# Delta rule of a hybrid decoder step: when the next tile's decay, the gate rows, z's second chunk and the solved blocks come

## The chip, the cores and the metric

One core of one Trainium2 chip runs the whole program in one launch. The metric is the time of one execution in device microseconds (us), as the median of several runs. TensorE (PE) multiplies matrices, VectorE (DVE) and ScalarE (ACT) work elementwise and can read TensorE's results in PSUM, GpSimd (POOL) works elementwise on SBUF, and SyncE (SP) issues DMAs. Each engine takes its instructions in order; semaphores tie the engines together.

## The reference

The program is one inference step of a two-layer trunk: a layer with sparse attention, a layer with gated DeltaNet, an MLP behind each. Tokens are 512 of a prompt and 8 sequences of 8 new tokens. Only the DeltaNet layer is touched. Its core, per head (16 value heads, keys and values of width 128, state 128 x 128):

```python
gam = jnp.cumsum(gc, axis=-1)                      # gc: log decay per token, in a chunk
diff = gam[..., :, None] - gam[..., None, :]
decay = jnp.where(incl, jnp.exp(jnp.where(incl, diff, 0.0)), 0.0)
a_mat = jnp.where(strict, bc[..., :, None] * jnp.einsum('...id,...jd->...ij', kc, kc) * decay, 0.0)
tinv = lax.linalg.triangular_solve(eye + a_mat, jnp.broadcast_to(eye, a_mat.shape), left_side=True, lower=True)
value = tinv @ (vc * bc[..., None])
kcum = tinv @ (kc * (bc * jnp.exp(gam))[..., None])
qk = jnp.einsum('...id,...jd->...ij', qc, kc) * decay
def step(s, xs):                                   # over chunks
    u = val - kcm @ s
    o = qd @ s + qkm @ u
    s = s * gl + jnp.swapaxes(kd, -1, -2) @ u
...
o = o * lax.rsqrt(jnp.mean(o * o, axis=-1, keepdims=True) + RMS_EPS) * norm_w * jax.nn.silu(zh)
y = o.reshape(n, t, GDN_V_W) @ w_out               # z = x @ w_z, the output gate
```

The states that enter and leave (`state_ssm`, one per sequence and head) are inputs and outputs.

## The kernel before

The DeltaNet layer is two stages. `gdn_in_stage` projects, convolves and normalises q, k and v in 16 weight units (n = 0 to 15); beside that POOL inverts the 16 x 16 diagonal blocks of the first four heads (`block_inverses`, a generator whose steps it takes between other work). SP writes the solved blocks to DRAM with `block_inverses_out`, 16 DMAs, and loads the first four z weight units into the ring of four slots. A barrier ends the stage.

`gdn_stage` is the delta rule. It runs four passes, `hg` 0 to 3, of four heads each. A pass has four prompt tiles of 128 tokens, i = 0 to 3, and then the eight sequences as one block of 64 tokens. Tiles alternate between two sets of buffers and PSUM banks (0 to 2 for even tiles, 3 to 5 for odd ones); z's products take pairs of banks, pair 2 being banks 4 and 5 and pair 3 banks 6 and 7. Each engine's order is written out by hand, in one function per engine, with counters per tile for the steps.

A tile goes so:

- SP loads its gate rows (`rows_load`, 256 KB into `a`), the 16 x 16 inverses (`t_load`, `inverse_load`) and the grown gates (`grown_load`).
- POOL subtracts and masks (`decay_gaps`, L3397 and L3400) and scales keys and queries by the grown gates (`grown_keys`, L3412 and L3414).
- ACT takes exp of `a` (`decay`, L3853), copies the turned values out of PSUM (`values`, L3859), scales the turned keys (`late_keys`, L3864). exp, silu and sqrt come from different tables, which an ACT_TABLE_LOAD changes; copy and square need no change.
- TensorE turns values and multiplies keys and queries (`first_products`, L3519 and L3526), turns keys (`keys_turned`, L3533). DVE makes `a` from the products (`keys`, L4007 and L4011).
- `join` grows the inverse from 16 to 32 to 64 to 128 in steps that alternate between TensorE and DVE or ACT: p16 (L3545), q16 and s16 (L3552, L3556), p32 (L3562), q32 and s32 (L3567, L3571), p64 (L3576), s64 (L3582). Between q32 and p64 ACT copies (`joined_32`, L3871 and L3874), after s64 again (`joined_64`, L3879).
- `use` applies the tile with the state: keys by state (L3599), queries by state (L3605), value (L3617), state (L3622), output (L3628). ACT squares the output (`square`, L3887), DVE sums, TensorE turns it (L3639), ACT writes it out (`out`, L3897).

TensorE runs the use of tile i between the join steps of tile i+1 and the first products of tile i+2. In ACT's loop over i before the change the order is

```python
late_keys(w[i + 1]); root(*last); decay(w[i + 2])          # last: norm of tile i - 1
out(*last, hg, i - 1); joined_32(w[i + 1]); square(*norm_of(hg, i), hg, i)
values(w[i + 2]); joined_64(w[i + 1])
```

The keys of the next pass are multiplied in 32 x 32 blocks by TensorE (`block_keys`, L3076), copied by ACT (L3953), sent through DRAM by SP and inverted by POOL.

After the tiles come the sequences: `seq_front`, then products with the eight states of each head j (L3814), then for each j two products (L3834) that DVE adds to the state (L4198), which POOL has scaled before (L3494). DVE spreads values for them (`by_sequence`, L4180). At the end SP stores the 2 MB of states (L3335).

z, the gate, is projected in the same pass as filler for TensorE's waits: `z_products` yields 32 pieces of a pass, 4 chunks c of 8 pieces (L3730, each 4 records), of which the last 8 (c = 3) are left for the next pass's start, except in pass 3. `Z_PAIR` says which pair of banks a chunk uses, ACT's `silu_z` (L3926) empties it and counts `z_out`. In pass 0 there is no such rest, and `keep_busy` multiplies ones instead (L123).

Four of the 16 q and k chunks ("units" 12 to 15) are brought to unit length in this stage by DVE (`unit_length`: a reciprocal, L4068, and a product, L4070), in the order 12, 13, 15, 14.

## Time and profile before

| | |
|---|---|
| median of 3 runs | 2309.18 us (2308.81 to 2311.12) |
| profiled execution, its own time | 2311.1 us |
| its span, first to last instruction | 2309.4 us |
| TensorE busy | 2182.4 us, 94% of the span |
| POOL, DVE, ACT busy | 1124.2, 1008.4, 577.0 us |
| mean granted TensorE clock | 0.974 of full speed |
| delta-rule stage, first instruction to the next stage's | 1243.5 to 1736.1 us |

How to read it: busy time is the time in which an engine had an instruction running. TensorE's matmuls are pipelined, so 94% does not mean that it does 94% of what it could. The granted clock is 1.0 at 2.4 GHz and 0.5 at 1.2 GHz. Waits and timelines tell what an engine waited for before an instruction: the brackets at the end of a row give the idle time and the instruction that ended it. "x4" counts records of one line that stand together.

### The profile page before, as it was taken

How to read it: one execution, taken by the hardware profiler on the slowest of the kernel's cores; microseconds unless marked ns; L12 is line 12 of the kernel's file. 1: busy time of each engine (PE TensorE's matmuls, PEld its weight loads, DVE VectorE, ACT ScalarE, POOL GpSimd, SP SyncE). 2: the span in 40 equal slices, each digit the busy share in tenths (PEclk: the TensorE clock that was granted, in tenths of full speed). 3: DMA queues.
4: the chain of work that ended last, by engine and by line, in shares of the span. 5: the costliest groups of instructions: out<-in, count | busy, mean ns of one | idle time of the engine just before them, and what ended most of it. 6: DMA issues, size and time to landing. Idle time of an engine off the chain costs nothing. (4 is left out here: it accounts for less than half of the span.)

```text
span 2309.4 us, 33163 instructions
## 1 busy us (share of the span) xinstructions
PE 2182.4 (94%) x12590; PEld 1617.2 (70%) x12590; DVE 1008.4 (44%) x1879; ACT 577.0 (25%) x1292; POOL 1124.2 (49%) x1075
## 2 busy tenths in 40 slices
PE   9898999899999999999998898989899999999997
PEld 7675555476777777767775767676767767777776
DVE  5343676336330341357886544343443163313422
ACT  2103577501000000135554424343320010000011
POOL 3212555257654565365695243525237276644653
PEclk9999799999999999999999999999999999999999
DMA  9825001911212221432223314242303122122211
GB/s 331 223 77 184 1 2 45 327 63 66 73 59 99 80 74 73 144 90 75 68 74 73 89 42 133 54 131 56 124 24 132 73 92 73 55 76 107 73 73 41
DMA packets 125912, 216.47 MB, mean 94 GB/s; under 512 B 73602, under 2 KB 96002, under 8 KB 109762
## 3 DMA queue, kind: packets, MB, share of 16 engines
q1 hardware_dynamic: 119234, 197.13, 25.9%
q0 software_dynamic: 3088, 14.03, 1.8%
q10 hardware_dynamic: 3440, 3.25, 0.4%
q8 instruction: 102, 1.67, 0.3%
q14 instruction: 48, 0.39, 0.1%
HBM read 185.08 MB, written 37.55 MB: 96 GB/s over the span
## 5 line engine op out<-in xcount | busy, mean ns | idle before, releaser
L2014 PE MATMUL ps<-xn,ring 128*128 128x288 f32 x768 | 198.8, 407 | 5.4 <-DVE xn L2117 3.2
L2014 PE MATMUL ps<-hid,ring 128*128 128x288 f32 x768 | 192.8, 406 | 0.0
L2014 PEld LDWEIGHTS ps<-xn,ring 128*128 128x128 f32 x768 | 145.3, 190 | 48.3 <-DVE xn L2117 5.9
L2014 PEld LDWEIGHTS ps<-hid,ring 128*128 128x128 f32 x768 | 145.6, 190 | 40.7 <-ACT p L2051 0.8
L2097 POOL TENSOR_TENSOR prod<-prod,rstd 128x1152 f32<-128x1152 f32 x32 | 83.9, 2621 | 179.6 <-DVE prod L2181 163.3
L2051 ACT ACTIVATE p<-ps 128x288 f32<-128x288 f32 x48 | 19.7, 410 | 597.4 <-PE ps L2014 597.4
L3730 PE MATMUL ps<-xn,ring 128*128 128x288 f32 x512 | 149.2, 429 | 5.9 <-PE ps L3834 4.0
L1122 POOL TENSOR_SCALAR ring<-ring,fac 128x128 f32<-128x128 f32 (+2 forms) x96 | 92.2, 976 | 88.1 <-DVE fac L1551 88.1
L2014 PE MATMUL ps<-x_sum,wsum 128*128 128x288 f32 x512 | 130.5, 407 | 3.4 <-DVE x_sum L2121 1.9
L2071 POOL TENSOR_TENSOR wsum<-ring 128x512 f32<-128x512 f32 x64 | 81.9, 1279 | 99.9 <-DMA ring<-in_w_mlp 92.0
L2014 PE MATMUL ps<-hid_sum,wsum 128*128 128x288 f32 x512 | 128.4, 407 | 0.2
L3730 PEld LDWEIGHTS ps<-xn,ring 128*128 128x128 f32 x512 | 93.3, 196 | 44.6 <-issue 22.6
L2014 PEld LDWEIGHTS ps<-x_sum,wsum 128*128 128x128 f32 x512 | 96.8, 190 | 32.0 <-issue 3.2
L2014 PEld LDWEIGHTS ps<-hid_sum,wsum 128*128 128x128 f32 x512 | 96.9, 190 | 28.3 <-POOL ring L2072 1.9
L2899 DVE SCALAR_TENSOR_TENSOR x<-x,gi_convw 128x600 f32<-128x600 f32 x90 | 92.4, 1026 | 30.6 <-ACT x L2693 28.3
L2171 DVE TENSOR_TENSOR u<-p,ps 128x288 f32<-128x288 f32 x48 | 21.7, 452 | 169.1 <-PE ps L2014 169.1
L2162 DVE TENSOR_TENSOR u<-p,ps 128x288 f32<-128x288 f32 x48 | 21.8, 453 | 159.3 <-PE ps L2014 159.3
L2076 POOL TENSOR_TENSOR wsum<-ring,wsum 128x512 f32<-128x512 f32 x64 | 87.9, 1374 | 5.0
L2072 POOL TENSOR_TENSOR ring<-ring 128x512 f32<-128x512 f32 x64 | 89.1, 1392 | 0.0
L3397 POOL TENSOR_TENSOR gdn_tiles<-gdn_tiles,gdn_upto_tok 128x512 f32<-128x512 f32 x16 | 16.6, 1040 | 145.4 <-DMA gdn_tiles<-gate_rows_scratch 145.2
L2074 POOL TENSOR_TENSOR wsum<-wsum,ring 128x512 f32<-128x512 f32 x64 | 82.9, 1295 | 0.0
L1382 ACT ACTIVATE ring<-ps,nmax 128x128 f32<-128x128 f32 (+3 forms) x128 | 66.1, 523 | 58.3 <-DVE nmax L1499 58.3
(597 smaller groups left out, 4650.8 us busy)
## 6 DMA issues: line engine op xcount, KB each, us to landing
ring<-in_w_mlp SPq DMA_DIRECT2D x64, 1024.0 KB, 4.9
ring<-in_w_gdn_in SPq DMA_DIRECT2D x16, 1024.0 KB, 4.9
ring<-in_w_nsa_in SPq DMA_DIRECT2D x9, 1024.0 KB, 17.4
ring<-in_w_gdn_z SPq DMA_DIRECT2D x8, 1024.0 KB, 5.0
x<-in_seq_state SPq DMA_DIRECT2D x4, 2048.0 KB
out_seq_state<-x SPq DMA_DIRECT2D x4, 2048.0 KB, 12.1
ring<-in_w_gdn_out SPq DMA_DIRECT2D x8, 1024.0 KB, 5.6
out_win_old<-in_win_rows POOLq DMA_DIRECT2D x1, 8064.0 KB, 46.5
```

What stands on the lines that cost most here:

```text
L1122: nc.gpsimd.tensor_scalar(p, p, fac[:, job % 2, half, i:i + 1], None, ALU.mult).then_inc(scaled, 1)
L1382: nc.scalar.activation(prob[job % 3][half][:, p_at(i):p_at(i) + width(i)], S.ps[:, score_bank(k, half), 0:width(i)], ACT.Exp, bias=nmax[:, ...
L2014: mm = nc.tensor.matmul(S.ps[:, base + BANK[p], 0:HT], stationary(p, blk.units[pair // 4], pair % 4), moving(blk.kind, p, pair), start=pai ...
L2071: g.tensor_tensor(wsum[:, slot, 0], quad[:, slot, 2], quad[:, slot, 3], ALU.add).then_inc(w_summed, 1)
L2072: g.tensor_tensor(quad[:, slot, 2], quad[:, slot, 0], quad[:, slot, 2], ALU.subtract).then_inc(w_summed, 1)
L2074: g.tensor_tensor(wsum[:, slot, 1], wsum[:, slot, 0], quad[:, slot, 0], ALU.subtract).then_inc(w_summed, 1)
L2076: g.tensor_tensor(wsum[:, slot, 2], quad[:, slot, 1], wsum[:, slot, 1], ALU.subtract).then_inc(w_summed, 1)
L2097: g.tensor_tensor(prod[:, i % 2], prod[:, i % 2], S.rstd[:, 1:2, :].broadcast_to([128, 2, T]), ALU.mult).then_inc(normal, 1)
L2162: v.tensor_tensor(u2[:, n % 2], p1[:, n % 2], b, ALU.add).then_inc(u2_set, 1)
L2171: v.tensor_tensor(u3[:, n % 2], p1[:, n % 2], b, ALU.add).then_inc(u3_set, 1)
L2899: i = v.scalar_tensor_tensor(out=c_, in0=p[:, t:t + CV], scalar=tap(t), in1=c_, op0=ALU.mult, op1=ALU.add)
L3730: mm = nc.tensor.matmul(S.pairs[:, Z_PAIR[c], half, :], S.ring[:, unit % SLOTS, k * 256 + (c % 2) * 128:k * 256 + (c % 2) * 128 + 128], S. ...
```

## The change

All of it is in the order of work; no arithmetic and no size of a transfer changes.

- SP, `gdn_in_stage`: the 16 stores of the first solved blocks are issued after the third z unit is loaded, not after the fourth and the convolution's rows.
- SP, `gdn_stage`, passes 1 to 3: the wait for z's last chunk and the ring load go from the head of the pass to behind tile 2's gate rows and inverses. The store of the states no longer waits for z's chunk.
- z's chunk 1 uses pair 2 and chunk 2 pair 3; the waits of TensorE go with them. `first_products` waits for `silu_z` only for tile 1, and for chunk 1 instead of chunk 2.
- ACT: `late_keys(w[1])` goes ahead of the last silu of the pass before, `decay(w[i + 2])` goes behind the square and right ahead of `values(w[i + 2])`. At the end of a pass tile 0's decay goes behind a silu.
- POOL: the next pass's tile 0 is prepared between the second and third state, not before the first. At the start, two of eight scalings of x precede the tiles instead of three.
- TensorE: `block_keys` goes from between p16 and q16 to behind the state product; pass 0 has four ones products instead of six at one place.
- DVE: unit 13's reciprocal and product go between tile 0's join steps (`unit_length` is split).
- Two constants are written by name; their values stay (2 and 3).

```diff
@@ gdn_in_stage, sync
                 if u == 2:
                     conv_out(2, 4, 8, 14)
+                    sp.wait_ge(blank_out, 32)
+                    block_inverses_out(sp, blocks, place, 0)
             z.prefetched = True
             conv_out(3, 4, 6, 15)
-            sp.wait_ge(blank_out, 32)
-            block_inverses_out(sp, blocks, place, 0)
             sp.wait_ge(last_set, 32)
@@ gdn_stage
-        Z_PAIR = (3, 3, 2, 3)
+        Z_PAIR = (3, 2, 3, 3)
@@ sync
                 else:
-                    sp.wait_ge(zd.product, 4 * hg)
-                    ring_load(2 * hg + 3)
                     sp.wait_ge(seq_add, hg * 8)
                     sp.dma_start(S.out["seq_state"][hg - 1], seq_state).then_inc(seq_out, 16)
                 wait_step(sp, C[0], "pe", w[0].job, "p64")
                 rows_load(w[2])
                 t_load(w[2])
+                if hg:
+                    sp.wait_ge(zd.product, 4 * hg)
+                    ring_load(2 * hg + 3)
                 wait_step(sp, C[0], "pe", w[0].job, "value")
                 grown_load(w[2])
                 inverse_load(w[2])
@@ gpsimd
-            scaled(0, 3)
+            scaled(0, 2)
             for i in range(2):
                 decay_gaps(tile(0, i))
                 grown_keys(tile(0, i))
-            scaled(3, KD)
+            scaled(2, KD)
...
                 if hg < 3:
-                    for i in (1, 0):
-                        decay_gaps(tile(hg + 1, i))
-                        grown_keys(tile(hg + 1, i))
+                    decay_gaps(tile(hg + 1, 1))
+                    grown_keys(tile(hg + 1, 1))
                 wait_step(pool, Q, "pe", hg, "value")
                 pool.wait_ge(seq_in, 16 * hg + 16)
                 for j in range(4):
+                    if j == 2 and hg < 3:
+                        decay_gaps(tile(hg + 1, 0))
+                        grown_keys(tile(hg + 1, 0))
                     g.tensor_tensor(seq_state[:, j], seq_state[:, j], seq_total(S, hg, j), ALU.mult).then_inc(seq_decayed, 1)
@@ tensor, first_products
                     wait_step(pe, Q, "act", w.hg)
-                    pe.wait_ge(z_out, 4 * w.hg - 1)
+                    if w.i == 1:
+                        pe.wait_ge(z_out, 4 * w.hg - 2)
@@ tensor, z_products
-                            elif c == 2:
+                            elif c == 1:
                                 wait_step(pe, C[1], "vec", 2 * hg + 2)
                                 wait_step(pe, N[1], "act", 2 * hg + 2)
                             else:
-                                pe.wait_ge(z_out, 4 * hg + (1 if c == 1 else 2))
+                                pe.wait_ge(z_out, 4 * hg + (1 if c == 2 else 3))
@@ tensor, the passes
                 first_products(first)
-                pause(1, 6)
+                pause(1, 4)
...
                     next(used)
-                    if i == 0 and hg < 3:
-                        pe.wait_ge(z_out, 4 * hg)
-                        if hg == 2:
-                            pe.wait_ge(late_unit, LATE)
-                        block_keys(S, hg + 1, lambda i, kh: ...).then_inc(blocks.keys_mm, 1)
                     next(joins, None)
                     next(used)
                     next(joins, None)
...
                     next(used)
+                    if i == 0 and hg < 3:
+                        (the same five lines)
                     if last:
                         turn(last[0], last[2], last[3])
@@ scalar
                 joined_64(w[0])
+                late_keys(w[1])
                 if hg:
                     silu_z(hg - 1, 3)
                 for i in range(PT):
                     last = norm_before(hg, i) if i else None
-                    if w[i + 1]:
+                    if i and w[i + 1]:
                         late_keys(w[i + 1])
                     if last:
                         root(*last)
-                    if w[i + 2]:
-                        decay(w[i + 2])
...
                     square(*norm_of(hg, i), hg, i)
                     if w[i + 2]:
+                        decay(w[i + 2])
                         values(w[i + 2])
...
                 if hg < 3:
-                    for i in (1, 0):
-                        decay(tile(hg + 1, i))
+                    decay(tile(hg + 1, 1))
                 silu_z(hg, 1)
+                if hg < 3:
+                    decay(tile(hg + 1, 0))
                 out(*norm_of(hg, PT), hg, PT)
                 silu_z(hg, 2)
@@ vector
+            def unit_inverse(e):
+                v.reciprocal(late_root(S, e), late_root(S, e)).then_inc(late_inverse, 1)
+
             def unit_length(e):
                 c, at = unit_chunk(e), late_root(S, e)
-                v.reciprocal(at, at).then_inc(late_inverse, 1)
...
                 if hg == 0:
+                    unit_inverse(12)
                     unit_length(12)
-                    unit_length(13)
                 keys(w[0])
                 joins = join(w[0])
                 next(joins)
+                if hg == 0:
+                    unit_inverse(13)
                 next(joins)
                 keys(w[1])
                 next(joins)
+                if hg == 0:
+                    unit_length(13)
                 next(joins)
```

## Rows read from the trace of the kernel before

**Rows 1.** TensorE's waits, 1230 to 1740 us: total us, times, longest.
```profile
PE ps L3576 <- ACT gdn_tiles L3871: 15.8, 3, 5.6
PE ps L3545 <- ACT gdn_tiles L3864: 6.2, 3, 2.1
...
PE ps L3834 <- DVE x L4198: 4.9, 3, 3.1
...
PE ps L3519 <- ACT gdn_shared L3926: 2.6, 3, 0.9
...
PE ps L3730 <- ACT gdn_shared L3926: 2.0, 4, 0.5
```

**Rows 2.** Timeline of TensorE, pass 1, around tile 1's 64-join: start, us, what.
```profile
1404.73 1.02 PE L3576 MATMUL ps<-gdn_tiles 64*64 64x64 f32 x8 [4.86 <-ACT gdn_tiles L3871]
...
1410.71 0.68 PE L3545 MATMUL ps<-gdn_tiles 64*64 64x64 f32 x16 [0.38 <-DVE gdn_tiles L4011]
```

**Rows 3.** Timeline of TensorE, pass 0, the same place, and the block keys.
```profile
1272.40 0.76 PE L3076 MATMUL ps<-gdn_qkv 128*32 128x32 f32 x64
...
1279.36 0.68 PE L3576 MATMUL ps<-gdn_tiles 64*64 64x64 f32 x8
...
1283.76 0.68 PE L3545 MATMUL ps<-gdn_tiles 64*64 64x64 f32 x16 [0.38 <-DVE gdn_tiles L4011]
```

**Rows 4.** Busy time and granted clock (PEclk), pass 1, behind the wait.
```profile
1405.00:1408.00 3.00, 3.00 (x19) 2.88 (x18) 0.43 (x1) 1.44 (x3) 1.26 (x1) 0.50 0.24 71
```

**Rows 5.** Timeline of ScalarE, pass 1, tiles 1 and 2.
```profile
1388.39 0.63 ACT L3926 ACTIVATE gdn_shared<-ps 128x576 f32<-128x576 f32 x1
1388.92 1.11 ACT L3864 ACTIVATE gdn_tiles<-ps,cst 128x128 f32<-128x128 f32 x4
1390.05 1.28 ACT L3853 ACT_TABLE_LOAD   x1
1403.75 0.63 ACT L3853 ACTIVATE gdn_tiles<-gdn_tiles 128x512 f32<-128x512 f32 x1 [12.42 <-POOL gdn_tiles L3400]
```

**Rows 6.** Timeline of GpSimd, pass 1, tile 2's decay gap.
```profile
1401.34 1.04 POOL L3397 TENSOR_TENSOR gdn_tiles<-gdn_tiles,gdn_upto_tok 128x512 f32<-128x512 f32 x1 [43.59 <-DMA gdn_tiles<-gate_rows_scratch]
```

**Rows 7.** DMA issues, 1387.4 to 1389.8 us (pass 1): KB, us to landing.
```profile
out_seq_state<-x SPq DMA_DIRECT2D x1, 2048.0 KB, 12.3
...
gdn_tiles<-gate_rows_scratch SPq DMA_DIRECT2D x1, 256.0 KB, 12.9
```

**Rows 8.** DMA issues of 1268.5 to 1269.4 us, pass 0.
```profile
gdn_tiles<-gate_rows_scratch SPq DMA_DIRECT2D x1, 256.0 KB, 3.2
```

**Rows 9.** Timeline of TensorE, pass 1, first and third state product.
```profile
1470.28 1.13 PE L3834 MATMUL ps<-gdn_tiles 32*128 32x512 f32 x4
...
1480.44 1.13 PE L3834 MATMUL ps<-gdn_tiles 32*128 32x512 f32 x4
```

**Rows 10.** Timeline of TensorE, pass 3, first and third state product.
```profile
1709.13 1.13 PE L3834 MATMUL ps<-gdn_tiles 32*128 32x512 f32 x4
...
1716.23 1.13 PE L3834 MATMUL ps<-gdn_tiles 32*128 32x512 f32 x4
```

**Rows 11.** Timeline of VectorE, last state adds of pass 0, first of pass 1.
```profile
1365.76 1.29 DVE L4198 TENSOR_TENSOR x<-x,ps 128x512 f32<-128x512 f32 x2 [2.14 <-PE ps L3834]
...
1473.83 1.28 DVE L4198 TENSOR_TENSOR x<-x,ps 128x512 f32<-128x512 f32 x2 [3.31 <-POOL x L3494]
```

**Rows 12.** Timeline of VectorE, start of the stage.
```profile
1254.97 0.68 DVE L4007 TENSOR_TENSOR gdn_tiles<-ps,gdn_tiles 128x512 f32<-128x512 f32 x1
```

**Rows 13.** Timeline of ScalarE, start of the stage.
```profile
1250.67 0.63 ACT L3853 ACTIVATE gdn_tiles<-gdn_tiles 128x512 f32<-128x512 f32 x1 [5.49 <-POOL gdn_tiles L3400]
```

**Rows 14.** Timeline of ScalarE, pass 0, copies around tile 1.
```profile
1293.84 0.60 ACT L3859 ACTIVATE gdn_tiles<-ps 128x512 f32<-128x512 f32 x1 [0.59 <-PE ps L3519]
1295.34 0.38 ACT L3879 ACTIVATE gdn_tiles<-ps 64x256 f32<-64x256 f32 x1 [0.90 <-PE ps L3582]
```

**Rows 15.** Waits of SP's queue, 1239 to 1246 us.
```profile
SPq L115 <- PEq L115: 0.7, 1, 0.7
```

More of the change, by code:

```diff
@@ L3355, in _ @@
                     if hg == 0:
-                        sp.wait_ge(late_unit, 2)
+                        sp.wait_ge(late_unit, LATE_ORDER.index(13) + 1)
                     else:
@@ L3775, in _ @@
                     next(used)
-                    if i == 0 and hg < 3:
-                        pe.wait_ge(z_out, 4 * hg)
-                        if hg == 2:
-                            pe.wait_ge(late_unit, LATE)
-                        block_keys(S, hg + 1, lambda i, kh: S.ps[:, 6, 64 * i + 32 * kh:64 * i + 32 * kh + 32]).then_inc(blocks.keys_mm, 1)
                     next(joins, None)
@@ L3787, in _ @@
                     next(used)
+                    if i == 0 and hg < 3:
+                        pe.wait_ge(z_out, 4 * hg)
+                        if hg == 2:
+                            pe.wait_ge(late_unit, LATE)
+                        block_keys(S, hg + 1, lambda i, kh: S.ps[:, 6, 64 * i + 32 * kh:64 * i + 32 * kh + 32]).then_inc(blocks.keys_mm, 1)
                     if last:
@@ L3922, in silu_z @@
                 if n == 0:
-                    act.wait_ge(late_unit, 3)
+                    act.wait_ge(late_unit, LATE_ORDER.index(15) + 1)
                 if hg:
@@ L4154, in _ @@
                     if (hg, i) == (0, 2):
+                        unit_inverse(15)
                         unit_length(15)
@@ L4185, in _ @@
                 if hg == 0:
+                    unit_inverse(14)
                     unit_length(14)
```

## The prediction

> **What bounds the kernel now.** The delta-rule stage runs four passes (hg 0 to 3), in each four prompt tiles (0 to 3) and then the eight sequences. TensorE's order is written out by hand, so a wait in it moves everything behind it. I read first TensorE's own waits over this stage [rows 1]: the reader is to see that few lines carry the idle time, and that most of these occur three times, once in each pass after the first. The largest is L3576 (the 64-join of tile 1, "p64"), 15.8 us in three waits for ACT L3871.
>
> Second, TensorE in time: in pass 1, p64 starts after 4.86 us idle and the next tile's first join 5.98 us after that [rows 2]; in pass 0, with no wait, the same distance is 4.40 us [rows 3]. The difference, 1.58 us, is the granted clock: just after the idle stretch it is 0.50, the lower level, 1.2 GHz [rows 4]. So a long wait costs about a third more than its idle time.
>
> Third, who is late. ACT L3871 is a small copy that queues behind tile 2's decay (L3853). The decay waited 12.42 us for POOL [rows 5], POOL for its DMA of gate rows [rows 6], and that DMA took 12.9 us to land because SP issued it behind a 1 MB ring load and the 2 MB state store, which itself took 12.3 us [rows 7]. In pass 0, with nothing ahead of it, the same load lands in 3.2 us [rows 8].
>
> Fourth, the sequence states at the end of a pass: in pass 1 TensorE goes from its first state product (1470.28) to the third (1480.44) in 10.16 us [rows 9], in pass 3, which has no next tile to prepare, in 7.10 us (1709.13 to 1716.23) [rows 10]. In pass 1 VectorE's first add waits 3.31 us for POOL [rows 11], which does both decays of the next pass before the first state.
>
> Fifth, the stage's start: VectorE's keys of tile 0 (L4007) begin at 1254.97, right behind two length units [rows 12], though the decay that they need was there at 1250.67 + 0.63 = 1251.30 [rows 13].
>
> **The change part by part** (us, summed over the stage).
>
> Gate rows ahead, decay behind the copy. SP no longer holds the state store until z's product is through; it can go when the last state add is done, at 1367.05 (1365.76 + 1.29 [rows 11]). The rows were issued at about 1388.4 (1401.34 - 12.9 [rows 6, 7]), 21 us after that, so the store's 12.3 us are over by then even if p64 comes some us earlier. The ring load goes behind tile 2's rows. So I take the 3.2 us landing. ACT does the decay after the copies, so p64 waits for neither: 15.8 saved [rows 1], and the slow clock behind it, 3 x 1.58 = 4.7 [rows 2, 3]. Were the rows late again, the decay would hold the value copy behind it instead, 2.4 a pass. That is worked out so: rows issued at 1388.4 that land 3.2 later are masked by 1393.9 (1.04 [rows 6] and some 1.3); p64 without its wait runs at 1399.9 (1404.73 - 4.86 [rows 2]), and the decay is due some 1.3 behind it, so 7.3 of the 9.7 (12.9 - 3.2) are covered. What is queued behind the moved ring load on SP are the grown rows and inverse of tile 2; they are issued after tile 0's value product and have a whole tile of cover.
>
> Tile 1's keys before silu. L3545 waits 6.2 in three for ACT's late keys L3864, which stand behind one silu [rows 1, 5]. They start at 1388.92 where the silu starts at 1388.39 [rows 5]; swapped, they gain 0.53 a pass, 1.6. The remaining wait of 1.5 comes from the 64-join copy ahead of both, which stays. Bounds: 1.6, and 1.6 + 3 x 1.5 if the shorter wait no longer lowers the clock; I take the first, since the state loop too loses 3.06 around waits of 0.9 ((4.9 - 3.1)/2 [rows 1]), most of it clock.
>
> The first products' wait for silu (2.6 in three, 0.87 each) is dropped for tile 0; the wait moves to z's last chunk behind these products, which cover it: 2.6 saved. In pass 3 nothing stands between z's third and fourth chunk, which now share a pair of banks: the same wait, 0.87, is new there. Bounds 0.6 (the silu alone [rows 5]) and 2.4 (with a clock fall of 1.5 more). On z's second chunk, moved to the other pair, the wait of 0.5 a pass goes: 2.0 saved [rows 1]. Its new wait, for tile 3's output copy, comes before the silu in ACT's order, so it is met.
>
> Tile 0's decay into the state loop. POOL's first state is scaled two instructions earlier (1.04 for the gap [rows 6], somewhat more for the mask), 2.3 of the 3.31 that VectorE waits [rows 11]. In passes 1 and 2 this should bring the 10.16 to the 7.10 of pass 3: 2 x 3.06 = 6.1 saved [rows 9, 10]. In pass 0 VectorE's own length unit is in front and stays; nothing. Bounds 0 to 6.1; I take 6.1, as pass 3 shows the loop without the decays. The third state now waits for the decay, but TensorE's third product is 10 us in, POOL's third state about 8.5. ACT's silu, exp, silu there adds two table loads a pass, while ACT waits for TensorE's turn.
>
> Start of the stage. Half of unit 12 and 13's work leaves the front. At most 1254.97 - 1251.30 = 3.7 is gained before the decay limits [rows 12, 13]; but the second unit's reciprocal comes back between two join steps, partly beside tile 1's products, and may open a new gap there that lowers the clock (1.5). Two ones products fewer shorten TensorE's filler so that it can follow. Bounds 1.5 to 3.7; I take 3.0. POOL's rows land at about the time when its third scale ended, so scaling two instead of three gives 0.3 at most, inside this.
>
> Costs. The block keys (L3076, 0.76 [rows 3]) leave a place where TensorE waits for VectorE anyway and go to one where it doesn't: 3 x 0.76 = 2.3 (bounds 0 and 2.3). The decay behind the square needs exp's table (1.28) and itself 0.63 [rows 5] on a path where ACT has 0.59 and 0.90 to spare [rows 14]: 0.4 left at least, 1.3 if only the first gap counts, and I take 0.55, near the lower, as the copy's reader runs later still. It applies to tile 1's turn in four passes and tile 0's in three: 3.9 (bounds 2.9 and 9.1).
>
> The Trainium skill speaks against this part: "ScalarE: Activation LUTs", section "What ACT_TABLE_LOAD costs", adds a drain of about 1.38 us to each load of 1.28. By it the seven loads would cost 9.7 more and the sum would be 19. The rows show the load at 1390.05, right as the keys end (1388.92 + 1.11) [rows 5], with no drain before it; the trace decides.
>
> Early store of solved blocks: SP at the stage's start waited 0.7 for TensorE [rows 15], so SP's 16 stores weren't what ended the stage before; nothing gained, and z's fourth unit, now behind them, is not used before pass 1. If TensorE had been ready, they would give 0.7 at most.
>
> Sum: 15.8 + 4.7 + 1.6 + 2.6 + 2.0 + 6.1 + 3.0 - 2.3 - 3.9 - 0.9 = 28.7. The profiled execution took 2311.1, 1.9 over the median 2309.2; the sum is a difference inside the stage and is taken off the median: 2280.5.
>
> **The rivals.**
> A, as above: 2280.5.
> B, the gate rows are as late as before or the state loop keeps its pace: TensorE's wait returns at the value copy (3 x 2.4 = 7.2) or the 6.1 is missing. For it: the rows still follow the 2 MB store on one queue; against it, the store starts so much earlier. 2287 to 2288, both 2294.
> C, the clock stays up after the shortened waits before tile 1's first join: 4.5 more, 2276. For it: those waits fall by a quarter; against it, waits of 0.9 sufficed in the state loop.
> D, slower. ACT now holds the value copy and the 64-join copy of the next tile behind the decay, which is in the path of every tile. Its input has 7.3 us of cover; each us beyond costs one us in every pass. To use up 28.7 the rows would have to land 7.3 + 28.7/3 = 16.9 us later than at 3.2, at 20.1; from there the time passes 2309. Against it: the latest in this stage is 12.9, with 3 MB ahead [rows 7]. At 24 us: 2321.
> E, the change doesn't do what it says, the waits only change their line: TensorE's copies, turns and keys wait for the same ACT, so the 20.5 of p64 go and return as waits at keys and first joins, with the 6.1 missing too: within 5 us of before, 2305 to 2309.
> F, each exp load on the path stops ACT for twice its row, 1.28 more: 7 x 1.28 = 9.0, 2289.5. Against it: ACT's instructions stand close around the load at 1390.05 [rows 5]. The Trainium skill's page named above is where such a rule stands.
>
> **How the numbers follow.** A 0.60, B 0.16, C 0.11, D 0.05, E 0.05, F 0.03. A's own range by the bounds: gains lower by up to 1.5 (start) and 1.5 (last wait), higher by 0.7 and 2.3: 2277 to 2284. With B's single cases, C and F, and with costs at 9.1 (5 more), the range that leaves out D, E, both of B together and little of the rest is 2271 (C with its bounds) to 2293. A measurement of this kernel tells 0.2% (4.6 us) from no change. Faster: A, B, C, F and part of E, 0.91; same: the rest of E, 0.04; slower: D, 0.05.
>
> **What would show it.** In the profile after: L3576's 15.8 gone, and with it the half clock behind; tile 2's rows landing in 3 to 4 us in passes 1 to 3, and the state store issued before p64; L3545 still waiting about 1.5 three times; exp loads behind the square and waits of about 0.5 at L3533 or L3545; the state loops of passes 1 and 2 at about 7 us; the first join of the stage near 1254 instead of 1256.87; a new wait near 0.9 before z's last chunk in pass 3. Wrong it would be if ACT's value copy (L3859) waits for the decay and TensorE for it, or if the state loop keeps its 10 us.

## The result and the profile after

| | before | changed |
|---|---|---|
| median | 2308.99 us (2307.80 to 2311.12, 4 runs) | 2270.40 us (2264.56 to 2273.84, 4 runs) |
| ratio | | 0.9829, 95% interval 0.9804 to 0.9854 |
| the same kernel in two later series | 2307.20, 2307.57 | 2275.69 and 2274.63; 0.9869 (0.9850 to 0.9888) and 0.9862 (0.9847 to 0.9877) |

The forecast was 2280.5, a gain of 28.7 us. Measured were 38.6 us in the first series and 31.5 and 32.9 in the later ones. The first series lies 0.6 us below the lower end of the forecast's range (2271 to 2293), the two later ones inside it. The signs and the places were right, the sum was too small by 3 to 10 us.

In the shown execution 10.5 us of the difference lie ahead of the delta-rule stage, which begins at 1234.24 and not at 1244.75 us, and 37.4 inside it: from its first product to the next stage's first it takes 454.1 us after (1234.24 to 1688.36) and 491.5 before (1244.75 to 1736.23).

TensorE's waits over the stage, of the changed kernel (us in total, times, longest). Its line numbers are up to 13 higher: L3545 is now L3549, L3576 is L3580, L3834 is L3838, L3864 is L3868:

```profile
PE ps L3549 <- ACT gdn_tiles L3868: 4.6, 3, 1.5
PE ps L3556 <- DVE gdn_tiles L4025: 4.0, 7, 0.9
...
PE ps L3537 <- ACT gdn_tiles L3863: 3.0, 7, 0.4
...
PE ps L3838 <- DVE x L4211: 2.4, 1, 2.4
...
PE ps L3734 <- ACT gdn_shared L3930: 1.1, 2, 0.8
```

Against [rows 1]: p64's 15.8 us are gone, and so is the wait of the first products for silu. The wait for tile 1's late keys is 1.5 and not 2.06, as forecast. New are the wait for the value copy behind the exp load (L3537, 0.4 in seven turns) and longer ones at q16 (L3556). TensorE in pass 1, around tile 1's joins, and in pass 3 ahead of z's last chunk:

```profile
1368.48 0.68 PE L3580 MATMUL ps<-gdn_tiles 64*64 64x64 f32 x8
...
1372.45 0.68 PE L3549 MATMUL ps<-gdn_tiles 64*64 64x64 f32 x16 [1.52 <-ACT gdn_tiles L3868]
...
1380.61 0.68 PE L3580 MATMUL ps<-gdn_tiles 64*64 64x64 f32 x8
...
1383.79 0.44 PE L3537 MATMUL ps<-cst,gdn_qkv 128*128 128x128 f32 x2 [0.42 <-ACT gdn_tiles L3863]
...
1677.59 2.66 PE L3734 MATMUL ps<-xn,ring 128*128 128x288 f32 x10 [0.83 <-ACT gdn_shared L3930]
```

From p64 of tile 0 to p64 of tile 1 it is 12.13 us (1368.48 to 1380.61); before it was 19.10. Who made room for that: SP's issue of tile 2's rows, GpSimd behind them, and the landing times of that stretch:

```profile
1350.94 0.37 SPq L3333 DMA_DIRECT2D out_seq_state<-x  x1
1369.18 0.33 SPq L3306 DMA_DIRECT2D gdn_tiles<-gate_rows_scratch  x1
...
1372.71 1.04 POOL L3398 TENSOR_TENSOR gdn_tiles<-gdn_tiles,gdn_upto_tok 128x512 f32<-128x512 f32 x1 [28.78 <-DMA gdn_tiles<-gate_rows_scratch]
...
out_seq_state<-x SPq DMA_DIRECT2D x1, 2048.0 KB, 6.3
...
gdn_tiles<-gate_rows_scratch SPq DMA_DIRECT2D x3, 256.0 KB, 3.5
```

The state store is issued 18 us ahead of the rows and over in 6.3 (12.3 before [rows 7]); the rows land in 3.5, not 12.9. ScalarE in the same place:

```profile
1371.24 1.11 ACT L3868 ACTIVATE gdn_tiles<-ps,cst 128x128 f32<-128x128 f32 x4
1372.24 0.64 ACT L3930 ACTIVATE gdn_shared<-ps 128x576 f32<-128x576 f32 x1
...
1380.72 0.60 ACT L3891 ACTIVATE x<-ps 128x512 f32<-128x512 f32 x1 [0.53 <-PE ps L3632]
1381.33 1.28 ACT L3857 ACT_TABLE_LOAD   x1
1382.62 0.63 ACT L3857 ACTIVATE gdn_tiles<-gdn_tiles 128x512 f32<-128x512 f32 x1
1383.16 0.58 ACT L3863 ACTIVATE gdn_tiles<-ps 128x512 f32<-128x512 f32 x1
```

Between the late copies and the 32-join copies ACT is idle for 6 us; the decay that could run there now runs behind the square. The state loop of pass 1, first to third product, takes 6.99 us (10.16 before [rows 9], 7.10 in pass 3 [rows 10]):

```profile
1444.46 1.13 PE L3838 MATMUL ps<-gdn_tiles 32*128 32x512 f32 x4
...
1451.45 1.13 PE L3838 MATMUL ps<-gdn_tiles 32*128 32x512 f32 x4
```

### The profile page after: what moved, and what is told of

Its sections match the earlier page's. It is cut to its first block and busy times, and to the rows that moved or that the text cites. A ratio compares the mean times of both kernels' runs of the same rounds, so it can differ in the third digit from the quotient of the medians.

```text
span 2262.9 us, 33160 instructions
## 1 busy us (share of the span) xinstructions
PE 2156.3 (95%) x12586; PEld 1600.4 (71%) x12586; DVE 1007.3 (45%) x1879; ACT 582.7 (26%) x1298; POOL 1125.2 (50%) x1075
## 5 line engine op out<-in xcount | busy, mean ns | idle before, releaser
L2162 DVE TENSOR_TENSOR u<-p,ps 128x288 f32<-128x288 f32 x48 | 21.8, 454 | 159.3 <-PE ps L2014 159.3
L1382 ACT ACTIVATE ring<-ps,nmax 128x128 f32<-128x128 f32 (+3 forms) x128 | 66.1, 523 | 55.3 <-DVE nmax L1499 55.3
L2474 POOL TENSOR_TENSOR x<-gi_prod,rstd 128x1024 f32<-128x1024 f32 (+1 forms) x16 | 36.7, 2293 | 69.6 <-DVE gi_prod L3011 65.3
```

Of the source, the lines that this page charges most:

```text
L1382: nc.scalar.activation(prob[job % 3][half][:, p_at(i):p_at(i) + width(i)], S.ps[:, score_bank(k, half), 0:width(i)], ACT.Exp, bias=nmax[:, ...
L2474: eng.tensor_tensor(p[:, first:last, 3:3 + TP], prod[:, first:last, 0:TP], S.rstd[:, 1:2, 0:TP].broadcast_to([128, m, TP]), ALU.mult).then ...
```

## The experiments

Medians of kernels in one series are compared with each other; finer things are read from stage lengths and stretches in the profiles, since executions differ by several us ahead of the stage (the first experiment).

**The changed kernel, twice more.**

> The changed kernel once more, nothing edited. In its first profile the delta-rule stage begins 10.5 us earlier than in the kernel before (first product at 1234.24 against 1244.75), although little of the diff runs ahead of the stage. Theory 1, chance: the clock's falls ahead of the stage differ from execution to execution; then the stage begins some us later here (1236 to 1245) and the median is 2268 to 2274, while the stage's own length, 454.1 us from its first product to the next stage's first, stays within 2 us. Theory 2, the diff does it (solved blocks stored earlier): the stage begins at 1233 to 1236 again, and so it does in each kernel with the early store.

> The changed kernel unedited, beside the next kernel on one chip. Theory: 2268 to 2277, the stage 454 to 456 us.

Measured: 2275.69 and 2274.63 us, the first above its 2268 to 2274. The stage begins at 1245.57 and 1242.07 and takes 454.7 and 458.5. So theory 2 is wrong: the same program starts the stage anywhere from 1234 to 1246. Most of the 10.5 us were chance: 6.8 of them stand before any changed line has run, where the stage ahead begins (TensorE's first L2664 at 959.6 us in the shown execution, 967.5 and 963.9 in the repetitions, 966.4 in the kernel before). What differs is the granted clock. Busy time by engine (PE, PEld, DVE, ACT, POOL), then the granted clock, DMA share and GB/s, of the shown execution in its first 600 us:

```profile
0.00:300.00 300.00, 277.45 (x1422) 194.54 (x1423) 143.81 (x364) 87.80 (x229) 94.24 (x162) 0.95 0.49 157
300.00:600.00 300.00, 286.20 (x2103) 183.58 (x2102) 155.86 (x400) 118.43 (x338) 164.04 (x143) 1.00 0.29 104
```

and of the repetition, with the same work:

```profile
0.00:300.00 300.00, 276.71 (x1393) 194.45 (x1393) 140.36 (x347) 84.29 (x219) 90.98 (x159) 0.93 0.49 157
300.00:600.00 300.00, 286.92 (x2100) 181.16 (x2097) 159.06 (x411) 121.78 (x348) 161.57 (x143) 0.98 0.29 103
```

The expected stage length held once and not the second time; the reason is in the next experiment.

**Late keys of tile 1 back behind silu.**

```diff
-                late_keys(w[1])
                 if hg:
                     silu_z(hg - 1, 3)
                 for i in range(PT):
-                    if i and w[i + 1]:
+                    if w[i + 1]:
                         late_keys(w[i + 1])
```

> The changed kernel with one edit undone: ACT's late keys of tile 1 stand behind z's last silu again. Theory of the prediction: the wait at the first join of tile 1 goes from 1.5 to 2.06 us in three passes, 1.6 us slower. Rival (the clock): a wait of 1.5 us leaves the clock up in two of three passes and one of 2.06 lowers it in all three; then 1.6 + 2 x 1.5 = 4.6 us slower, and p64 of tile 0 to p64 of tile 1 takes 13.3 to 14 us in each of passes 1 to 3, where the changed kernel takes 12.13, 13.38 and 11.44.

Measured: 2278.82 us, 3.1 more than the changed kernel in the same series. The stage takes 461.5, which is 7 us longer than in the first two profiles of the changed kernel and 3 longer than in the third. p64 of tile 0 to p64 of tile 1 takes 14.94, 14.96 and 14.24 us, where the changed kernel with the clock up takes 12.13, 12.13 and 11.44: 8.4 in all, of which 1.6 is idle time and 6.8 the clock. TensorE in pass 2, and the clock there (the column behind the five engines):

```profile
1494.36 1.12 PE L3549 MATMUL ps<-gdn_tiles 64*64 64x64 f32 x16 [2.06 <-ACT gdn_tiles L3868]
```

```profile
1494.00:1495.00 1.00, 0.64 (x12) 0.67 (x14) 0.00 (x0) 0.26 (x2) 0.49 (x1) 0.50 1.20 451
...
1498.00:1500.00 2.00, 2.00 (x10) 1.77 (x12) 0.84 (x2) 0.00 (x0) 0.00 (x0) 0.50 0.00 0
```

The rival holds, and for this stretch its price was still too low; the medians (3.1 us) lie between the two. I looked at the clock behind this wait in passes 1 to 3 of every profile, these runs' and the kernels' below. Behind waits of 2.06 us it fell to 0.50 in 13 of 15 (three of three in the kernel before); behind waits of 1.52 in 9 of 21: one, one and two of three in the three executions of the changed kernel; behind waits of 0.3 in none of 6. The three passes of one execution need not be independent: in one kernel all three fell. A fall costs 1.2 to 2.6 us in this stretch. In the shown execution it fell in pass 2 alone, at 1481:

```profile
1480.00:1481.00 1.00, 0.88 (x30) 0.88 (x32) 0.22 (x2) 0.00 (x0) 0.97 (x1) 1.00 0.99 418
1481.00:1482.00 1.00, 1.00 (x13) 0.89 (x10) 0.90 (x3) 0.00 (x0) 0.95 (x1) 0.55 0.61 254
1482.00:1483.00 1.00, 1.00 (x7) 1.00 (x5) 0.21 (x1) 0.00 (x0) 0.31 (x1) 0.50 0.04 16
```

**SP's part alone, in the kernel before** (only the `@@ sync` part of the diff: the wait for z's chunk and the ring load behind tile 2's rows).

> The kernel before with SP's part alone: in passes 1 to 3 the wait for z's last chunk and the ring load go behind tile 2's rows; ACT's order is as before. Theory 1 (the rows alone were late, the decay's place does not matter): the rows land 3.5 us after their issue, POOL takes 2.3 more, and ACT decays them some 2 us before the 32-join; p64's 15.8 us of waiting go and the slow clock behind them, 20 us faster, 2285 to 2289, with none of the 4 to 6 us that the decay behind the square costs. Theory 2 (both parts are needed): p64 of tile 1 still waits 1 us or more in each pass, and the gain is under 15 us.

Measured: 2286.37 us, 0.9903 (0.9875 to 0.9931), the stage 466.1. Theory 1 holds: the row of p64's wait is gone. ACT's decay, at its old place, waits 1.12 us for GpSimd and is still 3.17 us ahead of the 32-join:

```profile
1397.98 0.63 ACT L3854 ACTIVATE gdn_tiles<-gdn_tiles 128x512 f32<-128x512 f32 x1 [1.12 <-POOL gdn_tiles L3401]
1401.78 0.27 ACT L3872 ACTIVATE gdn_tiles<-ps 32x128 f32<-32x128 f32 x1 [3.17 <-PE ps L3568]
```

So the rows' place in SP's queue is worth some 22 us by itself, two thirds of the change. (Its late keys wait 2.06 us, and here the clock stayed up in two of three passes; why here and not in the kernel before stays open.)

**ACT's part alone, in the kernel before.**

```diff
-                    if w[i + 2]:
-                        decay(w[i + 2])
...
                     if w[i + 2]:
+                        decay(w[i + 2])
                         values(w[i + 2])
```

> The kernel before with ACT's part alone: the decay of tile i + 2 stands behind the square, ahead of the value copy; the rows are as late as before (12.9 us to land). Theory of the prediction (rival B worked out): p64 no longer waits, but the value copy behind the decay does, 2.4 us in each of three passes, and the exp load costs 3.9 to 6; so 20.5 - 7.2 - 5 = 8 us faster, 2299 to 2301. Rival E (the waits only change their line): within 3 us of before.

Measured: 2299.04 us, 0.9956 (0.9941 to 0.9970), 9.65 us faster. Rival B's mechanism, worked out in the prediction, appears, with waits of 2.3 to 2.9 us in the three passes where 2.4 was worked out:

```profile
PE ps L3533 <- ACT gdn_tiles L3859: 9.6, 7, 2.9
```

With the rows late, the decay's new place gives about half of what the rows' early issue gives (9.65 of 22), and the rest of the wait comes back at the value copy.

**The decay back at its old place, in the changed kernel.**

```diff
                         root(*last)
+                    if w[i + 2]:
+                        decay(w[i + 2])
...
-                        decay(w[i + 2])
                         values(w[i + 2])
```

> The changed kernel with ACT's decay of tile i + 2 back at its old place, ahead of the output copy and of the 32-join copies; the rows still come early. Theory of the prediction (the exp load behind the square is a cost of 0.55 in seven turns, 3.9 us): 4 to 6 us faster, since the waits of 0.4 before the turned keys and of 0.84 before q16 go and POOL is done before ACT comes to it (rows land in 3.5 us, POOL takes 2.3 more). Rival (the place of the decay is what removed p64's wait): p64 of tile 1 waits again in passes 1 to 3, 1 us or more each, and the time is the same or slower.

Measured: 2268.20 us against 2275.69 of the changed kernel in the same series, 7.5 faster where 4 to 6 were expected; the stage takes 448.9 against 454.7. The stretches that hold the moved exp load, p64 of tile 1 to p64 of tile 3 in four passes, sum to 106.6 us, and to 109.2 to 110.4 in the three profiles of the changed kernel: the load behind the square costs 2.6 to 3.9 (3.9 forecast). Of the rest, 1.4 us is the clock, which did not fall behind the late keys here and fell once in that profile of the changed kernel. p64 does not wait. So the new place gained nothing once the rows were early.

**Tile 0's decay back ahead of the states** (GpSimd and ACT prepare both tiles before the first state, as before).

> The changed kernel with the decay of the next pass's tile 0 undone on POOL and ACT: both tiles' gaps and grown keys ahead of the first state, both decays ahead of z's second silu. Theory of the prediction: the loop over the states goes from 7.0 back to 10.2 us in passes 1 and 2, 6.1 us in all, and pass 0 is as in the changed kernel (11.6), as VectorE's length unit is in front there. Rival: pass 0 loses too, 1.7 us more (13.3 as before), so that the stage goes from 454.5 to 462 us.

Measured: 2282.68 us, the stage 468.6: 14 us longer than in the first two profiles of the changed kernel, more than either theory. Waits of TensorE in the state loops, the second product of pass 1, and the clock behind it:

```profile
PE ps L3836 <- DVE x L4208: 6.8, 3, 3.7
```

```profile
1458.21 1.99 PE L3836 MATMUL ps<-gdn_tiles 32*128 32x512 f32 x4 [1.52 <-DVE x L4208]
```

```profile
1460.00:1464.00 4.00, 3.70 (x9) 2.53 (x8) 3.92 (x4) 0.00 (x0) 3.40 (x2) 0.50 0.96 295
1464.00:1468.00 4.00, 3.81 (x9) 1.38 (x8) 1.21 (x2) 0.00 (x0) 0.00 (x0) 0.50 0.00 0
```

From first to third product it is 14.17, 11.41 and 10.23 us in passes 0 to 2, against 11.60, 6.99 and 7.00 in the shown execution of the changed kernel. The waits grew by 4.4 in all (6.8 for 2.4), 1.5 in each of passes 1 and 2; the rest is the clock: in pass 1 TensorE is busy for 7.5 of the 8 us from 1460 to 1468 at the lower level. Pass 1 is slower here than in the kernel before (10.16), so this profile may price the part too high. Pass 0 loses too, so the rival's point holds. There VectorE is in front, and two of its instructions ahead of the second product take longer beside GpSimd's work: unit 14's product (1.74 us for 1.26) and the spread (`by_sequence`, L4189 here and L4192 in the changed kernel), which meets a scaling of the states here:

```profile
1343.76 2.36 DVE L4189 TENSOR_TENSOR gdn_tiles<-gdn_tiles,cst 64x512 f32<-64x512 f32 x1
```

and in the changed kernel, where GpSimd has turned to tile 0's gap by then, a shorter instruction:

```profile
1336.91 1.03 POOL L3398 TENSOR_TENSOR gdn_tiles<-gdn_tiles,gdn_upto_tok 128x512 f32<-128x512 f32 x1
...
1337.01 1.48 DVE L4192 TENSOR_TENSOR gdn_tiles<-gdn_tiles,cst 64x512 f32<-64x512 f32 x1
...
1339.61 0.67 DVE L4192 TENSOR_TENSOR gdn_tiles<-gdn_tiles,cst 64x512 f32<-64x512 f32 x1
```

**The early store of solved blocks alone, in the kernel before.**

> The kernel before with one edit: the 16 stores of the solved blocks are issued behind the third z unit, as in the change. Theory of the prediction: nothing gained, 0.7 us at most; 2308 to 2309, the stage's first product 10.8 us behind the last unit sum (L2612) as before. Rival: SP's stores held the end of the stage before; then this distance falls from 10.8 to 8.8 us, as in the profile of the changed kernel, the first products run at the full clock (0.63 us for L3519, not 1.09), and the median is 2306 to 2307.

Measured: 2306.72 us, 0.9995 (0.9983 to 1.0007): by the median it cannot be told from nothing, and the rival's 2 us are not excluded. The profiles decide. From the last unit sum (L2612) to the stage's first product it is 8.8 to 9.0 us in 8 of the 11 profiles with the early store and 10.5 in the other three; in the three kernels with the late store it is 10.4 to 10.8. Those three 10.5 are executions whose clock fell at the sums, so that TensorE itself was late. With the late store and the clock up, TensorE stands idle longer. ACT's part alone:

```profile
1244.25 1.09 PE L3519 MATMUL ps<-cst,gdn_qkv 128*128 128x128 f32 x4 [4.38 <-issue]
```

and the changed kernel:

```profile
1234.24 0.63 PE L3523 MATMUL ps<-cst,gdn_qkv 128*128 128x128 f32 x4 [2.44 <-issue]
```

SP's waits at that place in the kernel before, with a row that the prediction did not use:

```profile
SPq L115 <- PEq L115: 0.7, 1, 0.7
SPq L2414 <- PEq L2414: 0.2, 1, 0.2
```

and in the changed kernel:

```profile
SPq L2414 <- PEq L2414: 2.0, 1, 2.0
SPq L115 <- PEq L115: 0.7, 1, 0.7
```

L115 is 0.7 in both and tells nothing. At the barrier L2414 SP waited 2.0 us for TensorE after; with the late store the row is 0.2 in all three kernels, whether TensorE then stood idle for 2.7 us or for 4.4. So SP was last before and is out of the way now. The store is worth 0.3 us where the clock falls at the sums (10.8 to 10.5) and some 1.7 where it stays up (10.4 to 10.7 against 8.8 to 9.0).

**The start undone** (units 12 and 13 both ahead of tile 0's keys, three scalings, six ones products).

> The changed kernel with the start undone: both length units 12 and 13 ahead of tile 0's keys, three scalings of x ahead of the tiles, six ones products instead of four. Theory of the prediction: the stage's first product to p64 of tile 0 takes 3.0 us longer than the changed kernel's 18.8 to 19.2. Rival (nothing opens between the join steps, and the clock stays up): 4 us or more longer, up to 23.2 as before.

Measured: from the first product to p64 of tile 0 21.55 us, against 18.8 to 19.2: 2.4 to 2.8 longer, near the forecast's 3.0. VectorE's keys of tile 0 end at 1254.64 (1253.51 + 1.13), and the first join waits for them, as it did before; but here the clock stays up behind that wait. The kernel with the early store alone has this start too, and it reaches p64 of tile 0 after 20.31 us, also with the clock up there. Most of the 1.2 us between the two is unit 13's product on VectorE, which takes 0.76 us where it starts just ahead of GpSimd's grown keys, and 1.84 where it starts just behind them (first the kernel with the early store alone, then this one):

```profile
1252.81 0.76 DVE L4070 SCALAR_TENSOR_TENSOR gdn_qkv<-gdn_qkv,rstd 128x576 f32<-128x576 f32 x1
1252.83 1.87 POOL L3412 TENSOR_TENSOR gdn_tiles<-gdn_tiles,gdn_qkv 128x512 f32<-128x512 f32 x1
```

```profile
1250.99 1.27 POOL L3413 TENSOR_TENSOR gdn_tiles<-gdn_tiles,gdn_qkv 128x512 f32<-128x512 f32 x1
...
1251.04 1.84 DVE L4077 SCALAR_TENSOR_TENSOR gdn_qkv<-gdn_qkv,rstd 128x576 f32<-128x576 f32 x1
```

So with the clock up the old start costs 1.1 to 2.8 us, by which of the two engines begins first. The median, 2272.77 against 2274.63, doesn't show it; it lies inside the scatter of 4 us.

**The block keys back between p16 and q16.**

> The changed kernel with the block keys back between p16 and q16. Theory of the prediction: they cost 0.76 us in each of three passes where they stand now and nothing there, 2.3 us faster. Rival: TensorE waits only 0.52 us at q16, so they cost 0.2 there too: 0.55 a pass, 1.6 us; p64 of tile 0 to p64 of tile 1 takes 11.6 us where the clock stays up, not 12.13.

Measured: p64 of tile 0 to p64 of tile 1 takes 11.43, 11.55 and 11.54 us in passes 0 to 2 (12.02, 12.13, 12.13 with the clock up): 0.58 a pass, 1.75 in all. The rival's 0.55 holds: the old place wasn't quite free. The median, 2272.31, again doesn't show it.

**Three edits together, twice.** The decay at its old place and the block keys at theirs, as above, and the late keys moved into the idle time ahead of the 64-join copy:

```diff
-                joined_64(w[0])
                 late_keys(w[1])
+                joined_64(w[0])
```

> The changed kernel with three edits: the decay of tile i + 2 at its old place on ACT, ahead of the output copy; the late keys of tile 1 ahead of the 64-join copy of tile 0, where ACT is idle for 3 us; the block keys at their old place between p16 and q16. From the profiles so far: 5.5 us for the decay (stage 448.9 against 454.4), 3 x 1.5 for the wait at the first join of tile 1 and up to 1.5 for the clock behind it, up to 1.8 for the block keys, less 3 x 0.4 if they wait for z's silu: the stage takes 442 to 444 us and the kernel is 10 to 12 us faster than the changed one, 2260 to 2265. Rival: VectorE's masks bind the same joins, and no more than the decay's 5.5 us is gained.

> The kernel with three edits (decay ahead of the output copy, late keys of tile 1 ahead of the 64-join copy, block keys at their old place) once more, beside the changed kernel on one chip. Theory: the 10 us that the stage is shorter (444.75 against 454.4) show in the medians, 2260 to 2266. Rival: the first run's median, 2262.2, was helped by a good start of the stage (1236 us), and the two differ by less than 5 us.

Measured: 2262.22 us, 0.9805 (0.9786 to 0.9825), and 2258.53, 0.9801 (0.9787 to 0.9816), in one series with the changed kernel's 2274.63: 16 us faster there, a little more than expected. The stage takes 444.75 and 445.00 us, just over the 442 to 444 expected and 9 to 14 less than in the three profiles of the changed kernel. ScalarE and TensorE in pass 2: the late keys are done at 1475.63, and tile 1's first join waits 0.30 us for TensorE's own queue:

```profile
1474.49 1.14 ACT L3868 ACTIVATE gdn_tiles<-ps,cst 128x128 f32<-128x128 f32 x4
1477.44 0.38 ACT L3883 ACTIVATE gdn_tiles<-ps 64x256 f32<-64x256 f32 x1 [1.81 <-PE ps L3586]
...
1477.71 0.68 PE L3549 MATMUL ps<-gdn_tiles 64*64 64x64 f32 x16 [0.30 <-PEq L3615]
```

It beats both kernels, and the clock behind this join stayed up in all six passes.

## Why the prediction was too small, and what in it was right

The stage by stretches (us; passes 1 to 3 summed where nothing else is said), for the kernel before and three executions of the changed one, with the forecast's terms put where they belong:

| stretch | before | changed | forecast gain | measured gain |
|---|---|---|---|---|
| start to p64 of tile 0 | 23.2 | 18.8, 19.2, 19.0 | 3.0 | 4.0 to 4.4 |
| pass 0, p64 of tile 0 to tile 3 | 37.7 | 38.6, 38.8, 38.6 | -1.3 | -0.9 to -1.2 |
| p64 of tile 0 to tile 1 | 57.2 | 37.0, 37.1, 40.7 | 15.8 + 1.6 - 1.5 = 15.9 | 16.5 to 20.2 |
| p64 of tile 1 to tile 3 | 85.2 | 83.9, 82.4, 82.7 | 4.7 - 3.3 = 1.4 | 1.3 to 2.8 |
| p64 of tile 3 to first state, four passes | 153.9 | 151.8, 153.2, 151.9 | 2.0 | 0.7 to 2.1 |
| first state to next p64 of tile 0 | 107.3 | 96.1, 96.0, 97.5 | 6.1 + 2.6 = 8.7 | 9.7 to 11.3 |
| last states to the next stage | 27.1 | 28.0, 28.0, 28.0 | -0.9 | -0.9 |
| stage | 491.5 | 454.1, 454.7, 458.5 | 28.8 | 33.0 to 37.4 |

The step that failed is the price of the clock. TensorE's busy time (the first number behind the stage's length) and granted clock (0.95 and 0.98) in the stage, before and in the shown execution:

```profile
1244.75:1736.23 491.48, 436.20 (x4185) 328.92 (x4185) 223.30 (x469) 169.30 (x347) 191.41 (x238) 0.95 0.27 81
```

```profile
1234.24:1688.36 454.12, 420.01 (x4180) 316.04 (x4181) 223.37 (x469) 175.16 (x353) 192.74 (x238) 0.98 0.29 87
```

Idle time fell from 55.3 to 34.1 us, by 21.2 (21.8 and 22.0 in the repetitions); busy time fell by 16.2 (15.0 and 11.0), of which some 1 us is two ones products (four take 1.88 at the full clock) and the rest goes with the clock. Of the forecast's 28.8, the clock had 4.7 behind p64 and, if 2 x 0.9 of the state loops' 6.1 is waiting, 4.3 there: 9.0 in all, and 19.8 of idle time. So the waits were summed to some 2 us, and the clock was 1 to 6 us short.

Right: the mechanism of A. The late rows were the bound; p64's wait and the clock behind it went; z's chunk, the first products' silu, the wait in pass 3 and the state loops of passes 1 and 2 (3.17 a pass for 3.06) came as summed (they are read from the rows; z's pairs and the dropped waits for silu were not undone by themselves), and so, nearly, did the costs: 2.6 to 3.9 for the exp load (3.9), 1.75 for the block keys (2.3, its upper bound). Rival D's condition never came near: the rows landed in 3.5 us, not 20. F did not come: the value copy waited 0.4 us, and the load starts where the square ends (1380.72 + 0.60, load at 1381.33). The Trainium skill's page "ScalarE: Activation LUTs", section "What ACT_TABLE_LOAD costs", puts a drain of about 1.38 us to it; no row here has one. But one reason was wrong: the prediction gave p64's 15.8 to the early rows and the decay's new place together. SP's edit alone removes that wait; with the rows early the new place was not needed, and it cost.

Where it was too small:

1. The step that failed most was "Bounds: 1.6, and 1.6 + 3 x 1.5 if the shorter wait no longer lowers the clock; I take the first". Rival C is what happened, in part: the clock fell in one, one and two passes of three, not in all. TensorE's busy time in the third stretch, of which the forecast took nothing, fell from 33.6 us to 30.5 and 30.4 in the first two executions, 3 us of the excess of 4; in the third execution, whose falls cost 2.5 us each, it is 34.4, and the excess is 0.6. The argument, that waits of 0.9 sufficed in the state loop, took the fall for a property of the wait's length. It is a matter of chances, which a wait's length shifts.
2. "In pass 0 VectorE's own length unit is in front and stays; nothing." The loop of pass 0 went from 13.27 to 11.60, 11.53 and 12.84 us: VectorE's spread and unit 14's product, ahead of the second state product, are no longer slowed as much by GpSimd.
3. The start's 3.0 was idle time, with a fall of the clock as a risk. Undone, it costs 2.4 to 2.8, and 1.1 to 1.6 where VectorE's product is short, so the 3.0 is at the upper end. But before, the clock stood at 0.50 behind the first join's 2.02 us of waiting (eight products of L3526 at 1259.64 took 1.91 us, in the changed kernel 1.06), and that goes with the wait: 4.0 to 4.4 in all.
4. "SP's 16 stores weren't what ended the stage before; nothing gained". [rows 15] was misread: its 0.7 us is there whatever SP does. The store gives up to 1.7 us, ahead of the stage.
5. "The sum is a difference inside the stage and is taken off the median." The stage's own 33.0 to 37.4 us would give 2271.8 to 2276.2, inside the range. The first series' median lies 4 to 5 us below those of the two later series; its one profiled execution reached the stage early, and for the others that is likely but not shown. That the first median fell below the range is thus in part luck. Why the clock ahead of the stage differs between executions stays open.

## What to carry to other kernels

Ask of every late transfer what its queue holds ahead of it: one reordered issue on SP gave two thirds of this change, and the decay that was moved along with it cost some 3 us that nobody needed to pay. When a wait is followed by the lower clock, a shorter wait is worth more than its difference, by a chance; put both ends of the clock's cost in as cases with chances, and better remove the wait whole. A wait row is evidence only if it changes when the cause does: look for the same row where the cause is absent.

## What was unexpected of the hardware

TensorE's clock fell behind equal waits in some executions and passes and not in others (9 of 21 at 1.52 us, 13 of 15 at 2.06, none of 6 at 0.3), and a fall cost 1.2 to 2.6 us. In pass 1 of one kernel it stayed at 0.50 over a stretch in which TensorE was busy for 7.5 of 8 us.

VectorE's spread of 64 x 512 elements took 0.67 us right behind the end of a GpSimd instruction, 1.48 and 2.36 where one was running when it began; the 1.48 ended 0.55 us behind that instruction (1336.91 + 1.03 = 1337.94, and 1337.01 + 1.48 = 1338.49), the 2.36 likewise 0.54 (1345.58 and 1346.12). Such time stands in the instruction, not in a wait, so no list of waits names it. The Trainium skill, "SBUF — State Buffer", section "SBUF: two separate sides", says that the two engines share a pair of ports as an exclusive lock: whichever starts first has it for its whole instruction, and a VectorE instruction with two SBUF inputs takes part against a GpSimd instruction that reads SBUF. The rows agree, in both directions: unit 13's product took 1.84 us behind GpSimd's start and 0.76 ahead of it, and GpSimd's instruction beside it 1.27 and 1.87.
